# One 512-column product for high and low activations in the second block's up projection, with ScalarE and VectorE joining the halves

## The reference, cut to what matters

```python
h = rms_norm(x, ffn_norm_g[i])                       # 256 x 2048
val, gate = jnp.split(h @ w_up[i], 2, axis=-1)       # two times 256 x 5632
gate = causal_depthwise_conv_2(gate, conv_w[i], conv_b[i])   # three taps over the tokens
x = x + (val * jax.nn.gelu(gate, approximate=False)) @ w_down[i]
```

## Time and profile before

| | us |
|---|---|
| median of the three runs | 2674.3 |
| lowest and highest run | 2671.6, 2674.31 |
| span of the profiled execution (first to last instruction) | 2672.7 |

### The profile page before, as it was taken

How to read it: one execution, slowest core, us unless ns; L and a number is a source line. 1 busy time by engine, 2 the same in 40 slices (tenths; PEclk the granted TensorE clock), 3 DMA queues, 4 the chain that set the end, 5 groups by cost and what they waited for, 6 DMA issues and landing times.

```text
span 2672.7 us, 57540 instructions
## 1 busy us (share of the span) xinstructions
PE 2642.9 (99%) x22834; PEld 2628.9 (98%) x22834; DVE 1804.4 (68%) x2269; ACT 1274.7 (48%) x1548; POOL 249.9 (9%) x206
## 2 busy tenths in 40 slices
PE   9999999999999999999999999999999999999998
PEld 9999999999999999999999999999999999999998
DVE  5455555747888888864467999867576777775444
ACT  5334455345344444444455556554455555554442
POOL 1000000030000000001101665400100000000000
PEclk9999999999999999999999999999999999999999
DMA  7665556574555655556656555556656666666664
GB/s 256 193 199 175 150 161 182 169 213 148 173 195 196 196 194 189 196 191 203 192 168 200 174 163 157 155 183 200 194 183 195 196 194 193 191 190 197 195 191 141
DMA packets 137806, 496.71 MB, mean 186 GB/s; under 512 B 15425, under 2 KB 15425, under 8 KB 137537
## 3 DMA queue, kind: packets, MB, share of 16 engines
q1 hardware_dynamic: 137520, 494.20, 59.7%
q10 hardware_dynamic: 144, 0.52, 0.1%
HBM read 492.57 MB, written 2.10 MB: 185 GB/s over the span
## 4 chain that ended last, share of the span: by engine, by line
PE 89%; DVE 6%; DVEq 2%; ACT 1%; DMA 1%; issue 1%; ACTq 0%; SPq 0%
PE bank L432 86%; DVE w_lo L982 2%; PE ps_a L432 1%; PE ps_o L432 1%; PE ps_n L432 1%; DVE act_lo L1021 1%; PE ps_t L432 0%; DMA hT<-in_xT 0%; ACT w_hi L676 0%; DMA w_raw<-in_w_in 0%; ACT act_hi L742 0%; DVE hT L1046 0%; DVE pr L1309 0%; DVE rstd L1005 0%; DVEq L1299 0%
## 5 line engine op out<-in xcount | busy, mean ns | idle before, releaser
L982 DVE TENSOR_TENSOR w_lo<-w_raw,w_hi 128x1024 fp32r<-128x1024 f32 x928 | 1134.1, 1234 | 720.8 <-ACT w_hi L676 719.2
L676 ACT ACTIVATE w_hi<-w_raw 128x1024 fp32r<-128x1024 f32 x928 | 977.0, 1056 | 1185.9 <-PE bank L432 1045.3
L432 PE MATMUL bank<-act_hi,w_hi 128*128 128x256 f32 x5408 | 1275.3, 279 | 3.0 <-DVE gate_y L1350 2.5
L432 PE MATMUL bank<-act_lo,w_hi 128*128 128x256 f32 x5408 | 1264.9, 277 | 0.0
L432 PEld LDWEIGHTS bank<-act_hi,w_hi 128*128 128x128 f32 x5408 | 1014.9, 188 | 4.1 <-issue 2.7
L432 PEld LDWEIGHTS bank<-act_lo,w_hi 128*128 128x128 f32 x5408 | 1015.7, 188 | 0.7
L432 PE MATMUL bank<-act_hi,w_lo 128*128 128x256 f32 x5408 | 726.9, 277 | 2.7 <-DVE w_lo L982 2.7
L432 PEld LDWEIGHTS bank<-act_hi,w_lo 128*128 128x128 f32 x5408 | 666.6, 188 | 3.1 <-DVE w_lo L982 3.1
L432 PE MATMUL bank<-f_lo,w_hi 128*128 128x256 f32 x1408 | 327.9, 276 | 0.0
L432 PE MATMUL bank<-f_hi,w_hi 128*128 128x256 f32 x1408 | 327.9, 276 | 0.0
L432 PEld LDWEIGHTS bank<-f_lo,w_hi 128*128 128x128 f32 x1408 | 264.3, 188 | 0.0
(11 more groups left out here) (227 smaller groups left out, 1790.3 us busy)
## 6 DMA issues: line engine op xcount, KB each, us to landing
w_raw<-in_w_up SPq DMA_DIRECT2D x352, 512.0 KB, 4.2
w_raw<-in_w_in SPq DMA_DIRECT2D x252, 512.0 KB, 4.2
w_raw<-in_w_down SPq DMA_DIRECT2D x176, 512.0 KB, 4.2
w_raw<-in_w_out SPq DMA_DIRECT2D x64, 512.0 KB, 4.4
w_raw<-in_w_ple_gate SPq DMA_DIRECT2D x32, 512.0 KB, 4.5
w_raw<-in_w_branch_attn SPq DMA_DIRECT2D x16, 512.0 KB, 3.9
w_raw<-in_w_branch_a SPq DMA_DIRECT2D x8, 512.0 KB, 4.1
w_raw<-in_w_branch_b SPq DMA_DIRECT2D x8, 512.0 KB, 3.5
```

The costliest lines, as they stand in the source:

```text
L432: return pe.matmul(o, l, r, start=start, stop=stop, skip_group_check=True)
L676: act.activation(w_hi[:, k, 0:n, :], w_raw[:, k, 0:n, :], ACT.Copy).then_inc(hi_ready, 1)
L982: dve.tensor_tensor(w_lo[:, k, 0:n, :], w_raw[:, k, 0:n, :], w_hi[:, k, 0:n, :].bitcast(F32), ALU.subtract).then_inc(lo_ready, 1)
```

## The change: what it does

In up2 alone, one product takes `act_hi` and `act_lo` together as 512 moving columns for one load of `w_hi`. The two activation buffers become the two halves of one tile `act_x` (at the same addresses as before, 16 KB apart in each partition). Its result fills a whole PSUM bank: columns 0 to 255 are the sums with `act_hi`, 256 to 511 those with `act_lo`. Each slot has two banks (`twin`), one for each `c`; the products with `w_lo` add to the first half of each. `twin` takes the four banks that `bank` and `ps_a` had. ACT copies the second halves (128x512 numbers, 256 out of each of two banks) to `gate_y` or `val_y` in SBUF, and DVE adds them to the first halves in PSUM before its epilogue goes on as it was. The renaming of the other activation pairs (`y_x`, `f_x`, `p_x`, `x2_x`) changes no address and no instruction.

```diff
@@ build
-        act_hi = sb("act_hi", [P, DT, TOK], F32R)
-        act_lo = sb("act_lo", [P, DT, TOK], F32R)
+        act_x = sb("act_x", [P, 2, DT, TOK], F32R)
+        act_hi, act_lo = act_x[:, 0, :, :], act_x[:, 1, :, :]
...
-        bank = [ctx.enter_context(nc.psum_tensor(f"bank{i}", [P, 512], F32)) for i in range(2)]
-        ps_a = [ctx.enter_context(nc.psum_tensor(f"ps_a{i}", [P, 512], F32)) for i in range(2)]
+        twin = [ctx.enter_context(nc.psum_tensor(f"twin{i}", [P, 2, 2, TOK], F32)) for i in range(2)]
+        bank = [t[:, 0, :, :].rearrange("p h t -> p (h t)") for t in twin]
+        ps_a = [t[:, 1, :, :].rearrange("p h t -> p (h t)") for t in twin]
...
+        st_up2.halves, st_up2.half0 = True, 0
...
+        def halves_of(st, s):
+
+            of = twin[(st.group0 + s) % 2]
+            return of[:, :, 0, :], of[:, :, 1, :]
@@ tensor engine, stream
                         for t in range(n):
                             x = x0 + j * PIECE_KT + t
                             for c in range(2):
                                 o = ps[:, c * TOK:(c + 1) * TOK]
                                 w = w_hi[:, k, t, c * P:(c + 1) * P]
+                                if st.halves:
+
+                                    mm(twin[(st.group0 + s) % 2][:, c, :, :], w, both[:, :, x, :], j == 0 and t == 0, False)
+                                    continue
                                 mm(o, w, xh[:, x, :], j == 0 and t == 0 and c == 0, False)
                                 mm(o, w, xl[:, x, :], False, False)
...
-                                last = mm(ps[:, c * TOK:(c + 1) * TOK], w_lo[:, k, t, c * P:(c + 1) * P],
+                                o = halves_of(st, s)[0][:, c, :] if st.halves else ps[:, c * TOK:(c + 1) * TOK]
+                                last = mm(o, w_lo[:, k, t, c * P:(c + 1) * P],
                                           xh[:, x, :], False, j == st.pieces[s] - 1 and t == n - 1)
@@ scalar engine, gelu_gate
                 def ep(i, s):
+                    if st.halves:
+                        whole(st, i, s)
+                        if not (isinstance(i, int) and base + i == 0):
+                            act.wait_ge(f_ready if s else gate_act, base + i)
+                        act.activation((val_y if s else gate_y)[:, :, :], halves_of(st, s)[1], ACT.Copy
+                                       ).then_inc(half_kept, 1)
                     if s == 0:
                         return
@@ vector engine, conv and ffn
-                    x, y = ps[:, c * TOK:(c + 1) * TOK], dst[:, c, :]
+                    x, y = ps[:, c, :], dst[:, c, :]
...
-                        x, y = ps[:, c * TOK:(c + 1) * TOK - back], dst[:, c, back:]
+                        x, y = ps[:, c, 0:TOK - back], dst[:, c, back:]
...
                     whole(st, i, s)
-                    ps = bank_of(st, i, s)
-                    pair = ps[:, :].rearrange("p (c t) -> p c t", c=2)
+                    if st.halves:
+                        pair, y = halves_of(st, s)[0], (val_y if s else gate_y)
+                        dve.wait_ge(half_kept, st.half0 + 2 * i + s + 1)
+                        dve.tensor_tensor(pair, pair, y[:, :, :], ALU.add)
+                        dve.drain()
+                    else:
+                        pair = bank_of(st, i, s)[:, :].rearrange("p (c t) -> p c t", c=2)
                     if s == 0 or value_conv:
                         dve.tensor_tensor(pair, pair, over_tokens, ALU.mult)
                         dve.drain()
```

More of the change, by code:

```diff
@@ L103, in __init__ @@
         self.written_out = 1
+        self.halves = False
         self.pieces = [-(-kt // PIECE_KT) for _, _, kt, _ in slots]
@@ L201, in build @@
         z_b, t_b, l_b, sp_b, lw_b = over(80 * T, *((n, [P, BLK]) for n in ("z_b", "t_b", "l_b", "sp_b", "lw_b")))
-        y_hi, y_lo = over(KA * T, ("y_hi", [P, 8, T], F32R), ("y_lo", [P, 8, T], F32R))
+        y_x, = over(KA * T, ("y_x", [P, 2, 8, T], F32R))
+        y_hi, y_lo = y_x[:, 0, :, :], y_x[:, 1, :, :]
         mT, eT, tmp, sg, sq_x = over(
@@ L213, in build @@
         sq_sum = lambda n: squares_of(n)[:, 4:6, :]
[L215 to L218, removed]
+        f_x, gate_y, gate_g, val_y = over(
+            0, ("f_x", [P, 2, FT, T], F32R), ("gate_y", [P, 2, T]), ("gate_g", [P, 2, T]), ("val_y", [P, 2, T]))
+        f_hi, f_lo = f_x[:, 0, :, :], f_x[:, 1, :, :]
+        p_x, = over(2 * FT * T, ("p_x", [P, 2, 2, T], F32R))
+        p_hi, p_lo = p_x[:, 0, :, :], p_x[:, 1, :, :]
         proj2, kpad, vpad, s2_buf, small2, bc_pad, cz, rot, turns, vrot, scn, xs, pr, cz_t = over(
@@ L228, in build @@
         turn_t = tab[:, 2 * BLK + T:2 * BLK + 3 * T].rearrange("p (k t) -> p k t", k=2)
-        x2_hi, x2_lo, glu_v, glu_g = over(
-            PROJ2 * T, ("x2_hi", [P, 16, T], F32R), ("x2_lo", [P, 16, T], F32R), ("glu_v", [P, 4, T]), ("glu_g", [P, 4, T]))
-        bank = [ctx.enter_context(nc.psum_tensor(f"bank{i}", [P, 512], F32)) for i in range(2)]
-        ps_a = [ctx.enter_context(nc.psum_tensor(f"ps_a{i}", [P, 512], F32)) for i in range(2)]
+        x2_x, glu_v, glu_g = over(
+            PROJ2 * T, ("x2_x", [P, 2, 16, T], F32R), ("glu_v", [P, 4, T]), ("glu_g", [P, 4, T]))
+        x2_hi, x2_lo = x2_x[:, 0, :, :], x2_x[:, 1, :, :]
+        twin = [ctx.enter_context(nc.psum_tensor(f"twin{i}", [P, 2, 2, TOK], F32)) for i in range(2)]
+        bank = [t[:, 0, :, :].rearrange("p h t -> p (h t)") for t in twin]
+        ps_a = [t[:, 1, :, :].rearrange("p h t -> p (h t)") for t in twin]
         ps_t = [ctx.enter_context(nc.psum_tensor(f"ps_t{i}", [P, 512], F32)) for i in range(2)]
@@ L257, in build @@
         quarter_squared, quarters_added = sem("quarter_squared"), sem("quarters_added")
-        gate_act = sem("gate_act")
+        gate_act, half_kept = sem("gate_act"), sem("half_kept")
         gates_open = sem("gates_open")
@@ L284, in main_x @@
             return lambda j: (split_ready, first + j + 1)
-        act_x, f_x, p_x = (act_hi, act_lo), (f_hi, f_lo), (p_hi, p_lo)
         G = GROUP
@@ L306, in build @@
                         2, act_x, None, "dve")
-        st_branch = Stage("branch", branch1, 4, (y_hi, y_lo), lambda j: (split_ready, SPLIT["y1"] + 2), "dve")
+        st_branch = Stage("branch", branch1, 4, y_x, lambda j: (split_ready, SPLIT["y1"] + 2), "dve")
         st_out = Stage("out", pair("w_out"), 4, act_x, main_x(SPLIT["merged"]), "act")
@@ L316, in build @@
         st_in2b = Stage("in2b", tiles("w_in_2", ORDER_2[20:21]), 1, act_x, None, "dve")
-        st_glu = Stage("glu", [cols("w_glu_2", 4, 8, 0, k * G) for k in range(4)], 1, (x2_hi, x2_lo),
+        st_glu = Stage("glu", [cols("w_glu_2", 4, 8, 0, k * G) for k in range(4)], 1, x2_x,
                        lambda j: (split_ready, SPLIT["ssm_y"] + 1), "act")
         st_in2c = Stage("in2c", tiles("w_in_2", ORDER_2[21:]), 1, act_x, None, "dve")
-        st_branch2 = Stage("branch2", branch2, 2, (x2_hi, x2_lo), lambda j: (split_ready, SPLIT["ssm"] + 1), "dve")
+        st_branch2 = Stage("branch2", branch2, 2, x2_x, lambda j: (split_ready, SPLIT["ssm"] + 1), "dve")
         st_out2 = Stage("out2", pair("w_out_2"), 4, act_x, main_x(SPLIT["merged2"]), "dve")
@@ L434, in stream @@
             def stream(st, beside=None):
-                xh, xl = st.x
+                both, xh, xl = st.x, st.x[:, 0, :, :], st.x[:, 1, :, :]
                 def body(i, first):
@@ L1370, in ep @@
                     if s == 0:
-                        conv(gate_y, ps, w, b, 2 * i, tiles).then_inc(evacuated["dve"], 1)
+                        conv(gate_y, pair, w, b, 2 * i, tiles).then_inc(evacuated["dve"], 1)
                         return
                     if value_conv:
-                        conv(val_y, ps, w, b, 2 * i + FT, tiles).then_inc(evacuated["dve"], 1)
+                        conv(val_y, pair, w, b, 2 * i + FT, tiles).then_inc(evacuated["dve"], 1)
                         dve.drain()
```

## The result

| | kernel before | changed kernel |
|---|---|---|
| median of 14 runs each | 2671.4 us | 2677.0 us |
| lowest and highest | 2669.4, 2674.7 | 2674.4, 2679.4 |
| span of the profiled execution | 2672.7 us | 2677.6 us |

The ratio is 1.002, with an interval of 1.0012 to 1.0027: slower by about 0.2%, some 5.6 us. I had forecast 10 us less than before, and a range that ended at 2671.5 us. The forecast started from 2674.3 us, the median of three runs; fourteen runs put the kernel before at 2671.4, which changes nothing in the argument.

A forecast was written before the change was run, and what follows sets the result against it. PE's pace of products was taken to bound up2: 58 ns saved a piece, times 176 pieces, 10.2 us, less 0.2 for the first body, made 10.0 us, from 2674.3 to 2664.3 us; range 2657.5 to 2671.5.

The forecast's parts named there:

- What bounds the kernel, and where a gain could lie: Up2: PE never idle, 113.3 ns a product; the whole possible gain lies in the 6.6 ns not streaming.
- What a long stream pays: Up2: a 512-column product pays about 2.5 ns over its stream, 215.8 ns where the pair took 226.7.
- the counts: Profile after: 21,426 PE products instead of 22,834, 1408 with 512 columns; 44 ACT copies and 44 DVE sums.
- the durations on ACT and DVE: Profile after, up2: ACT copies of about 0.59 us and DVE sums of 0.69 us.
- the clock: Profile after: PE's granted clock in up2 stays at 1.00, which is 2.4 GHz.
- rival 2: Up2 products: the 6.6 ns are mostly no weight load; 3.5 us saved (2670.8) or nothing (2674.5); chance 0.17.
- What the short ones pay behind it: Up2: eight w_lo products behind long ones take 113.3 ns for one step and 117.5 for the seven others.
- The copy: ACT in up2: 44 copies out of PSUM, 591 ns each, covered, priced at nothing; 26 us if uncovered.
- the sum: DVE in up2's epilogues: 44 additions at 693 ns, covered, priced at nothing; 40 us if cover were gone.
- the first body: First loop body of up2: DVE's longer epilogue just frees the bank in time; 0.2 us taken, bounds 0 and 1.
- all of it goes with columns: Up2 products: the whole 6.6 ns goes with columns, so nothing is gained, 2674.5 us; no gain at all had chance 0.05.
- rival 3: Up2: long product slower than the pair, its columns from two runs 16 KB apart; 11.7 us more, 2686; chance 0.08.

The follow-up runs named there:

- the kernel at 16: Changed kernel with w_hi starting 16 words behind a 1 KB boundary instead of 48, w_lo where it was: 2705 us (4 runs), ratio 1.0146.

## Why the prediction was wrong

- **What bounds the kernel, and where a gain could lie**: the first is right: PE's pace is all that matters in up2, and the products' pace accounts for 4.7 of the spans' 4.9 us. The second is not: the 6.6 ns a product stood for columns read, and as many are read after the change.
- **"What a long stream pays"**: here it failed. I took a float32 pass of 256 columns, 216 ns, for the likeness of a float32r product of 512, because it "streams 213.3 ns, exactly as long". It is as long, but takes half as many columns in that time. At 0.84 ns a column the read from SBUF is in time; at full rate it isn't, and a column costs 0.443 ns at best. I equated two streams by duration where what bounds one of them goes by numbers read. The low clock of the earlier trace rows hides it in the same way: 214 ns for 256 columns. The term was 8 x 215.8 = 1726 ns a piece; measured 8 x 229.4 = 1835. The prediction's own sign of being wrong, long products 225 ns apart or more, is there; the counts, the durations on ACT and DVE and the clock are as it said.
- **The earlier trace rows misread**: 113 ns for a pass of 128 columns spoke for a floor a product, and there is one (111.7 ns with float32r weights). It stood beside 113.3 for 256 float32r columns, which goes with the read, and I took the likeness as evidence against rival 2. Two limits that lie 1.6 ns apart can't be told from one another by one length; a row with another length at full rate was what the prediction lacked.
- **"What the short ones pay behind it"**: the right kind, too large. Only behind the first w_lo product is the distance long (118 to 119 ns), then 113.3: 113.9 on average, 0.9 us in all in place of the 5.2 I took.
- **The copy, the sum, the first body**: priced at 0, 0 and 0.2 us, and right within what the runs can tell: the kernel with pairs in the new layout stands at 1.000. PE waited for nobody in up2, nor did it in the kernel that reads one number, whose pieces take 2.64 us.
- **Rivals**: "all of it goes with columns" was in rival 2 with a chance of 0.05 and was nearest to the ground; rival 3 had the right sign and the right place, a long product slower than the pair. Its reason, two runs 16 KB apart, was not it, and its price, 8.3 ns a product, was three times the 2.7 measured. What was measured is 226.7, as much as the pair, and 2.7 on top.
- **What those 2.7 ns are** is settled in part. They go away when PE reads one number (215.7, that is 2.4 over the stream), they are there with nothing beside PE, they don't depend on runs, banks or order, and they move with the start of the weights (226.7 to 234.3 alone, 232.9 in the kernel at 16) and with what ran before (229.4 or 233.5 at the same starts). That weight load and columns meet in reading SBUF fits most of this and is argued, not shown. Why long ones at 48 don't settle at 226.7 is open. Since these 2.7 ns are what makes the kernel slower than before, instead of as fast, that small loss is located but not explained; the gain that failed to come is.

## What to carry to other kernels

Before merging products to save per-product cost, find out whether the gap over the ideal goes with the product or with the columns: two lengths of the same type at the same clock, or one length reading a single number over and over, tell it in one run. Here full-rate float32r moving columns cost 0.443 ns each at best, by their read from SBUF, so fewer and longer products gave nothing. Columns of fewer bytes were faster by themselves (109.2 ns for 256 in bfloat16), but no piece that mixed them in averaged under the 2720 ns of before. An epilogue split between ACT and DVE cost nothing measurable where PE is the bound and, in the loop, the bank is wanted microseconds later.

## What had not been expected of the hardware

- Moving columns cost by their distance: 113.3 ns at best for 256 columns 4 bytes apart in either type, 226.7 at 8 bytes. At 16 bytes the types differ, 233.3 for float32r and 451.7 for bfloat16, the latter alike at a granted clock of 1.00 and of 0.50; why is open.
- Where weights start changes the pace of products, by up to 3% for 512 columns (226.7 to 234.3, nearly repeating 256 bytes on) and 6% for 256 (113.3 to 120.0).
- PE has a fast and a slow pace for the same products (113.3 and about 117.7) and can stay in the slow one for a whole stage when the weights start at another place: the changed kernel went from 2677 to 2705 us (four runs, 2690 to 2726) by moving one buffer 128 bytes.
